# Sample attention: old keys turned in place on VectorE, scores on 32x32 array tiles, pairs of sequences one by one

## The chip, the core and the metric

The kernel runs on one core of a Trainium2 chip. The metric is the device time of one execution in microseconds (us): the median of three runs. One further execution was recorded by the hardware profiler, and its rows are what is read here. The engines are TensorE (PE in the rows, its weight loads PEld), VectorE (DVE), ScalarE (ACT), GpSimd (POOL) and SyncE (SP), whose queue issues the large transfers.

## The reference, cut to what matters

The program is one inference step of a two-layer decoder trunk. Every layer projects its input, mixes tokens in three ways side by side (dilated attention A with 8 heads of 64, an RWKV recurrence B, and sliding-window attention C with 16 query heads on 2 key heads), projects back and applies a gated feed-forward block. There is one prompt of 256 tokens, and there are 8 sample sequences with 8 new tokens each. A sample sequence attends to cached keys and values that were loaded from memory. For mixer A these are 1280 cached positions that its branches reach; for mixer C the last 128 positions. In short, for each sample sequence and head:

```python
s = einsum(q, concat(cached_k, new_k)) * HEAD_DIM ** -0.5   # masked by branch and distance
p = softmax(s)                                              # C: with a learned sink
o = einsum(p, concat(cached_v, new_v))
```

## The kernel before

All engines are programmed by hand; a named semaphore stands for each hand-over, and each engine takes its instructions in the order in which they are written. A layer runs the input projections, the RWKV stage, the attention of the prompt (24 units, loop over `u`), the attention of the samples, the output projection `out` and the feed-forward block. Tokens stand in the free dimension of `pT` (256 prompt columns, then 64 of samples).

The sample attention takes the eight sequences in four pairs, q = 0 to 3. The cached keys of a pair lie in `cK[0]` and `cK[1]`, the values in `cV[0]` and `cV[1]`: 128 partitions (positions) x 10 blocks x 512 columns (8 heads of 64) in float32, loaded in three pieces, called quads, of 4, 4 and 2 blocks. The last pair's values go to `cK[0]` and to `cX`. `ckc` and `cvc` hold the C keys and values of 128 positions.

A score needs the head dimension on the partitions, but the cache brings positions there. So TensorE first turns the keys:

- `keys(q)`: `turn` transposes 128x128 blocks of `cK` against an identity into two PSUM banks (82 a pair, with the two of `ckc`), ScalarE's `key_tiles` copies them to `ktr` (eight buffers, 26 copies a pair), and `score` multiplies them by the queries `qdA`, in four column tiles of 32 side by side. Then come the new keys: `pT,qdA` and `pT,qdC` in the rows.
- VectorE's `scores(q)` scales and masks the PSUM result into `smA` and `smC` and takes the maxima `snm`; ScalarE's `exps(q)` makes the exponentials and their sums `ssu`.
- `probabilities(q)`: TensorE transposes `smA` and `smC`, ScalarE copies them to `ptA` and `ptC`.
- `values(q)`: TensorE multiplies the new values (`tk`), the C values (`cvc`) and the cached values (`cV`) by them; VectorE's `weighted(q)` scales the result into `om` and `omC`.
- `select(q)`: TensorE gathers `om` and `omC`, and VectorE's `outputs(q)` writes them to `pT`.

TensorE's order is keys(0), then for each q keys(q+1), probabilities(q), values(q). The `select` of a pair stands within the keys of a later one. Semaphores in the rows: `s_bS` scores of a pair are in PSUM; `s_smb` VectorE has read them; `s_bnm` maxima are there; `s_bex` exponentials are there; `s_pvq` a piece of the values is done; `s_ktp`, `s_ktc` a block is turned, copied; `s_sc` a group of scores is done; `s_cK0` and the like: a quad has landed.

SyncE issues the keys of a next pair quad by quad, as `s_ktp` counts up, and the values as `s_pvq` does.

Of the kernel before, what the change touches and what calls it, by code (L numbers as in the profile page):

```python
# [31 lines left out]
ALU = mybir.AluOpType  # L32
# [5 lines left out]
P = 128  # L38
# [136 lines left out]
def build(nc, I, O, at):  # L175
    ctx = ExitStack()
    with ctx:
# [82 lines left out]
        ktr = [place(f"ktr{i}", [P, 512], RW + 40960 + 2048 * i if i < 3 else RK + 2048 * (i - 3)) for i in range(8)]  # L260
# [28 lines left out]
        def C(name, rows=P, cols=None):  # L289
# [4 lines left out]
        names = """con con2 x x1 xh xlo par lora s0 cK0 cK1 cK2 cV0 cV1 cV2 w0 w1 wh wl mm ev gexp  # L294
            xtr xtc sq ssum nmm hh part
            zero shc sht shrc th sg z aa zexp aexp g gc ksq kss rkp rks clr expd abkr bon st stc
            tok tokc mixq RKs G Gc et Z Zc TZ TW TA TAc NV NVc TNV U Uc Sm SP Y Yc mz mk U1 U1c ux Se SF So Soc
            gn gnc ysq gv vr sd rn gsd grn xs keep kf cl drr bl vx Sov TT WZ rk2 sqd ssd finr hpp qp qp0 et0 E1 NT RB tnv rw rot rotc kv kvc qz qbd
# [20 lines left out]
        TURNS, GROUPS = 26, 7  # L319

        def group_of(g):
            return g // TURNS * GROUPS + min(g % TURNS // 4, GROUPS - 1)

# [4 lines left out]
        def keys_in(l, q, quad):  # L328

            return sem[f"cK{quad}"], (304 if quad == 2 else 288) * l + 64 * (q + 1)  # L330

        def values_in(l, q, quad):

            if q == LASTQ:
                return sem[f"cK{quad}"], (304 if quad == 2 else 288) * (l + 1)
            return sem[f"cV{quad}"], 32 * (3 - quad) * (LASTQ * l + q + 1)

# [22 lines left out]
        def _(sp):  # L360
# [75 lines left out]
            for l in range(DEPTH):  # L436
# [12 lines left out]
                sp.wait_ge(sem["zero"], 2 * l + 3)  # L449
# [17 lines left out]
                def cache(b, which, quad):  # L467

                    last = which == "V" and b // 2 == LASTQ
                    s = sem[f"c{'K' if last else which}{quad}"]  # L470
# [19 lines left out]
                for which in "KV":  # L490
                    for quad in range(3):
                        cache(0, which, quad)
                        cache(1, which, quad)
# [15 lines left out]
                def next_keys(q):  # L509
                    for quad in range(3):  # L510
                        sp.wait_ge(sem["ktp"], TURNS * (4 * l + q - 1) + (8 * (quad + 1) if quad < 2 else TURNS))
                        cache(2 * q, "K", quad)
                        cache(2 * q + 1, "K", quad)

                def next_values(q):
                    for quad in range(3):
                        if q < LASTQ:
                            sp.wait_ge(sem["pvq"], 3 * (4 * l + q - 1) + quad + 1)
                        else:
                            sp.wait_ge(sem["ktp"], TURNS * (4 * l + q) + (8 * (quad + 1) if quad < 2 else TURNS))  # L520
                        cache(2 * q, "V", quad)
                        if q < LASTQ:
                            cache(2 * q + 1, "V", quad)
                        elif quad == 2:
                            sp.dma_start(ckc[1][:], I["cache_c_v"][l, NB - 1].rearrange("r h d -> r (h d)")).then_inc(sem["cK2"], 16)
                next_keys(1)
                next_keys(2)
                next_values(1)
                next_keys(3)
                next_values(2)  # L530
                next_values(3)
# [7 lines left out]
            for tau, need in enumerate((1, 0, 2)):  # L539
# [14 lines left out]
        def _(pool):  # L554
# [9 lines left out]
            for l in range(DEPTH):  # L564
# [3 lines left out]
                pool.wait_ge(sem["pool"], l + 1)  # L568
# [18 lines left out]
                pool.memset(mkb[1][:], 0.0).then_inc(sem["mz"], 1)  # L587

                pool.wait_ge(sem["SF"], 4 * (l + 1))
                pool.wait_ge(sem["rope"], 9 * (l + 1))  # L590
                for i in range(4):
                    pool.memset(qp[i][:], 0.0).then_inc(sem["qp0"], 1)
                for u in range(24):

                    if u:
                        pool.wait_ge(sem["qp"], 24 * l + u)
                    else:
                        pool.wait_ge(sem["qp0"], 4 * (l + 1))
# [9 lines left out]
                z.then_inc(sem["qz"], 1)  # L608
                pool.wait_ge(sem["qz"], l + 1)
                pool.wait_ge(sem["rope"], 9 * (l + 1))  # L610
# [19 lines left out]
        def _(act):  # L630
# [155 lines left out]
            for l in range(DEPTH):  # L786
# [62 lines left out]

                for u in range(24 + 3):  # L850
# [24 lines left out]
                def key_tiles(q):  # L875
                    for t in range(TURNS):
                        if q == 1 and t in (4, 8):
                            exps(0, t == 4)
                        g = TURNS * (4 * l + q) + t
                        n = QUADS[t // 8][1] * P if t < 24 else P  # L880
                        take("ktp")
                        if g >= 8:
                            act.wait_ge(sem["sc"], group_of(g - 8) + 1)
                        act.activation(ktr[g % 8][:, 0:n], PS[:, 4 + g % 2, 0:n], ACT.Copy).then_inc(sem["ktc"], 1)  # L884

                def exps(q, first=None):

                    i = q % 2
                    if first in (None, True):
                        take("bnm")  # L890
                        act.activation(smA[i][:], smA[i][:], ACT.Exp, bias=snm[i][:, 0:1], accum_out=ssu[i][:, 0:1])
                    if first in (None, False):
                        for b2 in range(2):
                            act.activation(smC[i][:, b2], smC[i][:, b2], ACT.Exp, bias=snm[i][:, 1 + b2:2 + b2], accum_out=ssu[i][:, 1 + b2:2 + b2])
                        act.activation(ssk[i][:], snm[i][:, 1:3], ACT.Exp, bias=snk[:, 0:1]).then_inc(sem["bex"], 1)

                act.wait_ge(sem["snk"], 16 * (l + 1))
                key_tiles(0)
                for q in range(NB // 2):
                    if q < NB // 2 - 1:  # L900
                        key_tiles(q + 1)
                    if q == 0:
                        act.wait_ge(sem["out"], 16 * 12 * (l + 1))
                    for r in range(4):
                        take("pt2")
                        b0 = r if q == LASTQ else 6 + r % 2
# [11 lines left out]
                    if q < NB // 2 - 1:  # L918
                        exps(q + 1)

                act.wait_ge(sem["pvq"], 12 * l + 9)
                act.wait_ge(sem["ktp"], TURNS * 4 * (l + 1))
# [13 lines left out]
            act.wait_ge(sem["finr"], 1)  # L936
# [9 lines left out]
        def _(dve):  # L946
# [222 lines left out]
            def rwkv(l):  # L1169
                xk = xm[:, 4:8]  # L1170
                col = lambda r, f: par[:, r + f:r + f + 1]
                dve.wait_ge(sem["zero"], 2 * l + 2)
# [3 lines left out]
                for tau in range(3):  # L1176
# [40 lines left out]
                    for c in range(2) if tau < 2 else range(1):  # L1217
# [3 lines left out]
                        else:  # L1221
                            dve.wait_ge(sem["TAc"], 3 * (l + 1))
                            take("mz")
# [72 lines left out]
            def attention(l):  # L1296
# [20 lines left out]

                def scores(q):
# [5 lines left out]
                    for k in range(3):  # L1324
                        n = 512 if k < 2 else 256
                        stt(x[:, 512 * k:512 * k + n], PS[:, k, 0:n], SCALE, C("oldA")[:, 512 * k:512 * k + n], ALU.mult, ALU.add)
                    stt(x[:, 1280:1344], PS[:, 2, 256:320], SCALE, C("newA")[:, 64 * q:64 * q + 64], ALU.mult, ALU.add)
                    ps = PS[:, 3, 0:384].rearrange("p (b k) -> p b k", b=2)
# [5 lines left out]
                def weighted(q):  # L1334
# [7 lines left out]
                    stt(v3(om[:]), v3(PS[:, 6, 0:256]), ssu[i][:, 0:1], C("headof").unsqueeze(2).broadcast_to([P, 4, HD]), ALU.mult, ALU.mult)  # L1342
                    for b2 in range(2):
                        a = stt(omC[:, b2], PS[:, 7, b2 * P:(b2 + 1) * P], ssu[i][:, 1 + b2:2 + b2], C("headones"), ALU.mult, ALU.mult)
# [679 lines left out]
```

## Time and profile before

| what | value |
|---|---|
| median of 3 runs | 3399.21 us (3396.51 to 3399.39) |
| the profiled execution's own time | 3401.5 us |
| its span in the profile | 3399.6 us |
| TensorE busy | 3272.0 us, 96% of the span |
| VectorE busy | 1711.3 us, 50% |
| ScalarE busy | 1208.5 us, 36% |

The span is the time from the first to the last recorded instruction. Matmul ends are modelled, so a busy TensorE is not TensorE at its peak. The shares are averages over stages with different limits. The stage that the change touches stands once in each layer, in the first from 528.4 us on and in the second from 2201.8 us on.

### The profile page before, as it was taken

How to read it: one execution, taken by the hardware profiler on the slowest of the kernel's cores; microseconds unless marked ns; L12 is line 12 of the kernel's file. 1: busy time of each engine (PE TensorE's matmuls, PEld its weight loads, DVE VectorE, ACT ScalarE, POOL GpSimd, SP SyncE). 2: the span in 40 equal slices, each digit the busy share in tenths (PEclk: the TensorE clock that was granted, in tenths of full speed). 3: DMA queues.
4: the chain of work that ended last, by engine and by line, in shares of the span. 5: the costliest groups of instructions: out<-in, count | busy, mean ns of one | idle time of the engine just before them, and what ended most of it. 6: DMA issues, size and time to landing. Idle time of an engine off the chain costs nothing.

```text
span 3399.6 us, 60962 instructions
## 1 busy us (share of the span) xinstructions
PE 3272.0 (96%) x25078; PEld 3074.4 (90%) x25078; DVE 1711.3 (50%) x2269; ACT 1208.5 (36%) x1607; POOL 91.9 (3%) x209
## 2 busy tenths in 40 slices
PE   7999888999999999999999988889999999999998
PEld 6999755699999999999999986557999999999998
DVE  5455572355555454454545664714555544545544
ACT  3332256433322222222434313654422323323234
POOL 1000011000000000000000000100000000000000
PEclk9999889999999999999999998999999999999999
DMA  6552036765555554554564610577655545545454
GB/s 196 164 135 65 2 132 234 258 151 150 150 150 140 159 148 138 160 148 140 152 190 136 137 27 2 191 278 201 148 149 151 149 140 164 149 136 161 137 146 132
DMA packets 848704, 501.17 MB, mean 147 GB/s; under 512 B 96608, under 2 KB 823152, under 8 KB 848112
## 3 DMA queue, kind: packets, MB, share of 16 engines
q1 hardware_dynamic: 848108, 499.01, 51.7%
q8 instruction: 106, 1.74, 0.2%
q14 instruction: 38, 0.31, 0.0%
q10 hardware_dynamic: 452, 0.11, 0.0%
HBM read 485.71 MB, written 13.37 MB: 147 GB/s over the span
## 4 chain that ended last, share of the span: by engine, by line
PE 91%; DVE 4%; ACT 2%; issue 1%; DMA 1%; ACTq 0%; SPq 0%; DVEq 0%
PE PS L1435 87%; PE PS L1436 4%; ACT ktr L884 1%; ACT psm L855 0%; DVE psm L1303 0%; DVE wl L962 0%; ACT ppt L866 0%; DVE nm L1305 0%; ACT wh L641 0%; DVE S0T L1255 0%; DMA sink<-in_c_sink 0%; DVE rt L1080 0%; DMA raw<-in_w_out 0%; DVE WT L1183 0%; DMA raw<-in_w_in 0%
## 5 line engine op out<-in xcount | busy, mean ns | idle before, releaser
L641 ACT ACTIVATE wh<-raw 128x2048 fp32r<-128x2048 f32 (+1 forms) x408 | 711.7, 1744 | 1235.7 <-PE PS L1435 1214.2
L962 DVE TENSOR_TENSOR wl<-raw,wh 128x2048 fp32r<-128x2048 f32 (+1 forms) x408 | 848.9, 2081 | 400.2 <-ACT wh L641 399.6
L1435 PE MATMUL PS<-fh,wh 128*128 128x320 f32 x2816 | 870.6, 309 | 0.0
L1435 PE MATMUL PS<-fh,wl 128*128 128x320 f32 x2816 | 870.1, 309 | 0.0
L1435 PE MATMUL PS<-fl,wh 128*128 128x320 f32 x2816 | 870.1, 309 | 0.0
L1435 PEld LDWEIGHTS PS<-fh,wh 128*128 128x128 f32 x2816 | 528.5, 188 | 0.2
L1435 PEld LDWEIGHTS PS<-fl,wh 128*128 128x128 f32 x2816 | 528.5, 188 | 0.2
L1435 PEld LDWEIGHTS PS<-fh,wl 128*128 128x128 f32 x2816 | 528.5, 188 | 0.0
L1435 PE MATMUL PS<-hh,wh 128*128 128x320 f32 (+2 forms) x1696 | 521.3, 314 | 4.8 <-DVE wl L962 4.8
L1435 PE MATMUL PS<-hh,wl 128*128 128x320 f32 (+2 forms) x1696 | 513.5, 309 | 0.0
L1435 PE MATMUL PS<-hl,wh 128*128 128x320 f32 x1664 | 510.5, 310 | 0.0
L1435 PE MATMUL PS<-ah,wh 128*128 128x320 f32 x1408 | 435.7, 309 | 0.2 <-DVE wl L962 0.2
L1435 PE MATMUL PS<-al,wh 128*128 128x320 f32 x1408 | 435.1, 309 | 0.0
L1435 PE MATMUL PS<-ah,wl 128*128 128x320 f32 x1408 | 435.1, 309 | 0.0
L1435 PEld LDWEIGHTS PS<-hh,wh 128*128 128x128 f32 x1696 | 317.9, 191 | 8.6 <-DVE wl L962 5.2
L1435 PEld LDWEIGHTS PS<-hh,wl 128*128 128x128 f32 x1696 | 315.2, 189 | 0.0
L1435 PEld LDWEIGHTS PS<-hl,wh 128*128 128x128 f32 x1664 | 312.2, 188 | 1.4
L1435 PEld LDWEIGHTS PS<-ah,wh 128*128 128x128 f32 x1408 | 264.3, 188 | 0.8 <-issue 0.5
L1435 PEld LDWEIGHTS PS<-al,wh 128*128 128x128 f32 x1408 | 264.3, 188 | 0.0
L1435 PEld LDWEIGHTS PS<-ah,wl 128*128 128x128 f32 x1408 | 264.3, 188 | 0.0
L670 ACT ACTIVATE ge<-gt 128x320 f32<-128x320 f32 x88 | 41.5, 472 | 488.2 <-DVE gt L1002 488.2
L1002 DVE TENSOR_TENSOR gt<-PS,rsb 128x320 f32<-128x320 f32 x88 | 43.3, 492 | 224.7 <-PE PS L1435 224.6
(329 smaller groups left out, 2711.4 us busy)
## 6 DMA issues: line engine op xcount, KB each, us to landing
raw<-in_w_gate SPq DMA_DIRECT2D x88, 1024.0 KB, 5.6
raw<-in_w_up SPq DMA_DIRECT2D x88, 1024.0 KB, 5.6
raw<-in_w_down SPq DMA_DIRECT2D x128, 704.0 KB, 4.8
raw<-in_w_in SPq DMA_DIRECT2D x56, 1024.0 KB, 5.6
cK<-in_cache_a_k SPq DMA_DIRECT2D x80, 512.0 KB, 6.5
cV<-in_cache_a_v SPq DMA_DIRECT2D x60, 512.0 KB, 8.8
raw<-in_w_in SPq DMA_DIRECT2D x32, 512.0 KB, 5.3
raw<-in_w_out SPq DMA_DIRECT2D x32, 512.0 KB, 4.5
```

The source lines that it names most:

```text
L641: act.activation(wh[j][:, 0:kts], raw[j][:, 0:kts], ACT.Copy).then_inc(sem["wh"], 1)
L670: act.activation(ge[:], gt[:], ACT.Tanh, scale=0.5).then_inc(sem["gexp"], 1)
L884: act.activation(ktr[g % 8][:, 0:n], PS[:, 4 + g % 2, 0:n], ACT.Copy).then_inc(sem["ktc"], 1)
L962: tt(wl[j][:, 0:kts], raw[j][:, 0:kts], wh[j][:, 0:kts].bitcast(F32), ALU.subtract).then_inc(sem["wl"], 1)
L1002: tt(gt[:], PS[:, 0, 0:TOK], rsb[:], ALU.mult).then_inc(sem["ev"], 1)
L1435: mm = lambda out, lhsT, rhs, start=True, stop=True: pe.matmul(out, lhsT, rhs, start=start, stop=stop, skip_group_check=True)
L1436: tr = lambda out, x: pe.transpose(out, x, con[0:x.shape[0], at["ident"][0]:at["ident"][0] + x.shape[0]])
```

## The change

VectorE's new `turn(q)` transposes the loaded keys in place, in blocks of 32x32, with six instructions a pair (128x2048, 128x2048 and 128x1024 for each sequence). A 32x32 block then has 32 columns of a head on 32 partitions, and TensorE scores such blocks: a 32x32 tile of queries `qd` against 320 moving columns, with four row groups (`i`) times two column groups (`fh`), in four PSUM banks. The eight parts of a sum (four heads, two halves of a head) are accumulated in one bank. The queries have to lie on all four groups of 32 partitions: `query_rows(q)` brings them there by 16 small matmuls against the identity and eight ScalarE copies into `qd`, two buffers that GpSimd clears. The one for pair 0 stands ahead of the prompt attention.

```diff
+                def turn(q):
+
+                    for b2 in range(2):
+                        for quad, (k0, n) in enumerate(QUADS):
+                            dve.wait_ge(*keys_in(l, q, quad, b2))
+                            x = cK[b2][:, k0:k0 + n].rearrange("p k c -> p (k c)")
+                            dve.transpose(x, x).then_inc(sem["kt"], 1)
...
+                    old = lambda z: z[:, 0:1280].rearrange("p (k i c) -> p i k c", k=10, i=4)
+                    for r in range(4):
+                        stt(old(x)[:, r], PS[:, 4 + r, 0:320].rearrange("p (k c) -> p k c", k=10), SCALE, old(C("oldA"))[:, r], ALU.mult, ALU.add)
...
+                turn(0)
                 scores(0)
                 for q in range(NB // 2):
-                    if q:
-                        outputs(q - 1)
                     if q < NB // 2 - 1:
-                        scores(q + 1)
+                        turn(q + 1)
                     else:
                         split(start_of(l, "out"), 0, KT)
                     weighted(q)
+                    if q < NB // 2 - 1:
+                        scores(q + 1)
+                        outputs(q)
...
+                def query_rows(q):
+
+                    o = SEQ + 2 * TS * q
+                    for g in range(4):
+                        r = slice(32 * g, 32 * g + 32)
+                        for i in range(4):
+                            a = mm(PS[32 * i:32 * i + 32, 4 + g, 448:512].rearrange("p (f t) -> p f t", f=4), C("ident")[r, r], pT[r, QA:QA + 4, o:o + 2 * TS])
+                    a.then_inc(sem["ktp"], 1)
+                query_rows(0)
+                pe.wait_ge(sem["ktc"], 12 * l + 1)
                 for u in range(24 + 3):
...
                 def keys(q):
 
-                    for t in range(4):
-                        turn(q, t)
-                    take("qbd")
                     if q:
                         pe.wait_ge(sem["smb"], 4 * l + q)
-                    for group in range(GROUPS):
-                        for t in range(4 * group + 4, min(4 * group + 8, TURNS)):
-                            turn(q, t)
-                        if group == 3 and q >= 2:
-                            select(q - 2)
-                        score(q, group)
+                    window_keys(q)
+                    take("qbd")
+                    pe.wait_ge(sem["ktc"], 12 * l + 3 * q + 1)
+                    for b2 in range(2):
+                        pe.wait_ge(sem["kt"], 6 * (4 * l + q) + 3 * (b2 + 1))
+                        for h in range(4):
+                            for jj in range(2):
+                                for i in range(4):
+                                    r = slice(32 * i, 32 * i + 32)
...
+                                    for fh in range(2):
+                                        out = PS[64 * b2 + 32 * fh:64 * b2 + 32 * fh + 32, 4 + i, 0:320].rearrange("p (k c) -> p k c", k=10)
+                                        c0 = (4 * fh + h) * HD + 32 * jj
+                                        a = mm(out, qd[q % 2][r, b2, jj, fh, 32 * h:32 * h + 32], cK[b2][r, :, c0:c0 + 32], not (h or jj), h == 3 and jj == 1)
+                        a.then_inc(sem["sc"], 1)
...
-                keys(0)
                 for q in range(NB // 2):
+                    keys(q)
+                    if q:
+                        select(q - 1)
                     if q < NB // 2 - 1:
-                        keys(q + 1)
-                        probabilities(q)
-                    else:
-                        probabilities(q)
-                        select(q - 1)
+                        pe.wait_ge(sem["smb"], 4 * l + q + 1)
+                        query_rows(q + 1)
+                    probabilities(q)
                     values(q)
```

ScalarE's `key_tiles` goes. In its place are two copies of the turned C keys into `kcT` and, for the next pair, the eight of `query_rows`, both ahead of `exps(q)`. SyncE now asks for the next keys of a sequence when its scores are done (`s_sc`), in the order next_keys(q), next_values(q). The results of `values` move from PSUM banks 6 and 7 to banks 2 and 3. The rest renames semaphores.

Two places show how the order moves. The first is TensorE around the hand-over from a pair's keys to transposed probabilities. In the kernel before, at the end of pair 1's keys (`ktr`, `qdA_152`, `qdC_154` are of pair 1, `smA_165` of pair 0):

```order
L1435 MATMUL PS<-ktr_142,qdA_152 32x256
L1435 MATMUL PS<-ktr_143,qdC_154 128x128 [waits s_ktc]
L1435 MATMUL PS<-ktr_144,qdC_154 128x128
L1435 MATMUL PS<-pT,qdA_152 128x64 x4
L1435 MATMUL PS<-pT,qdC_154 128x64 x2
L1436 MATMUL PS<-con,smA_165 128x128 [waits s_bex]
L1436 MATMUL PS<-con,smA_165 128x128 x7
L1436 MATMUL PS<-con,smA_165 128x128 [waits s_ptd]
```

In the changed kernel, right behind the 128 tile matmuls of pair 1's old keys (`smA_162` is of pair 1, `om` and `omC` are of pair 0, `pT,con` is the query rows of pair 2):

```order
L1444 MATMUL PS<-pT,qdA_148 128x64 [waits s_ktc]
L1444 MATMUL PS<-pT,qdA_148 128x64 x3
L1444 MATMUL PS<-kcT_141,qdC_150 128x128
L1444 MATMUL PS<-pT,qdC_150 128x64
L1444 MATMUL PS<-kcT_142,qdC_150 128x128
L1444 MATMUL PS<-pT,qdC_150 128x64
L1444 MATMUL PS<-con,om 128x32 [waits s_om]
L1444 MATMUL PS<-con,om 128x32
L1444 MATMUL PS<-con,omC 128x64 x2
L1444 MATMUL PS<-pT,con 32x64 [waits s_smb]
L1444 MATMUL PS<-pT,con 32x64 x15
L1445 MATMUL PS<-con,smA_162 128x128 [waits s_bex]
```

Before, pair 0's probabilities stood behind the whole of pair 1's keys. Now a pair's probabilities stand behind its own scores, with only `select` of the pair before and the 16 matmuls of the query rows between them and the wait for the exponentials (`s_bex`).

The second place is VectorE after the maxima of a pair. In the kernel before, between the maxima of pair 1 (`snm_188`) and the scores of pair 2:

```order
L1331 TENSOR_REDUCE snm_188<-smA_166 128x1 [waits s_smb]
L1332 TENSOR_REDUCE snm_188<-smC_168 128x2
L1338 TENSOR_TENSOR ssu_189<-ssu_189,ssk_191 128x2 [waits s_bex,s_bnm]
L1339 RECIPROCAL ssu_189<-ssu_189 128x3 [waits s_dve]
L1342 SCALAR_TENSOR_TENSOR om<-PS,ssu_189,con 128x256 [waits s_pvq,s_dve]
L1344 SCALAR_TENSOR_TENSOR omC<-PS,ssu_189,con 128x128 x2
L1351 COPY pT<-PS 128x2x16 [waits s_sel,s_om]
L1351 COPY pT<-PS 128x2x16
L1354 COPY pT<-PS 128x8x8 x2
L1326 SCALAR_TENSOR_TENSOR smA_165<-PS,con 128x512 [waits s_pt2,s_bS,s_bo]
```

In the changed kernel, between the maxima of pair 0 (`snm_183`) and the scores of pair 1:

```order
L1339 TENSOR_REDUCE snm_183<-smC_163 128x2
L1323 STREAM_TRANSPOSE cK_139<-cK_139 128x2048 [waits s_cK00,s_bnm]
L1323 STREAM_TRANSPOSE cK_139<-cK_139 128x2048 [waits s_cK10]
L1323 STREAM_TRANSPOSE cK_139<-cK_139 128x1024 [waits s_cK20]
L1323 STREAM_TRANSPOSE cK_140<-cK_140 128x2048 [waits s_cK01]
L1323 STREAM_TRANSPOSE cK_140<-cK_140 128x2048 [waits s_cK11]
L1323 STREAM_TRANSPOSE cK_140<-cK_140 128x1024 [waits s_cK21]
L1345 TENSOR_TENSOR ssu_185<-ssu_185,ssk_187 128x2 [waits s_bex]
L1346 RECIPROCAL ssu_185<-ssu_185 128x3 [waits s_dve]
L1349 SCALAR_TENSOR_TENSOR om<-PS,ssu_185,con 128x256 [waits s_pvq,s_dve]
L1351 SCALAR_TENSOR_TENSOR omC<-PS,ssu_185,con 128x128 x2
L1333 SCALAR_TENSOR_TENSOR smA_162<-PS,con 128x10x32 [waits s_bS,s_om]
```

The six transposes of the next pair stand ahead of this pair's sums and weighted values, which stand ahead of the next pair's scores.

## Rows read from the trace of the kernel before

**Rows 1.** Page, the chain that ended last: shares of the span.

```profile
PE 91%; DVE 4%; ACT 2%; issue 1%; DMA 1%; ACTq 0%; SPq 0%; DVEq 0%
```

**Rows 2.** Stretches of the stage: us, then each engine's busy us, PEclk, DMA share, GB/s.

```profile
528.40:549.40 21.00, 18.68 (x147) 11.43 (x148) 0.00 (x0) 12.14 (x27) 0.00 (x0) 1.00 0.62 215
549.40:575.00 25.60, 21.25 (x149) 12.92 (x148) 4.29 (x8) 14.50 (x33) 1.93 (x12) 0.87 0.60 211
...
605.80:636.50 30.70, 27.91 (x267) 17.43 (x266) 6.18 (x17) 16.63 (x39) 0.00 (x0) 1.00 0.88 330
...
2201.80:2331.30 129.50, 114.04 (x1052) 70.57 (x1052) 25.01 (x60) 70.88 (x161) 3.85 (x24) 0.97 0.71 248
```

**Rows 3.** TensorE's timeline, one pair: start, us, operation, count, idle before and releaser.

```profile
584.47 1.09 PE L1436 MATMUL PS<-con,cK 128*128 128x128 f32 x8
...
598.92 0.53 PE L1435 MATMUL PS<-con,om 128*128 128x32 f32 x4
...
599.86 1.07 PE L1435 MATMUL PS<-ktr,qdA 128*32 128x512 f32 x8
...
603.92 0.71 PE L1435 MATMUL PS<-ktr,qdC 128*128 128x128 f32 x4
...
605.75 1.04 PE L1436 MATMUL PS<-con,smA 128*128 128x128 f32 x8
...
608.92 0.64 PE L1435 MATMUL PS<-tk,ptA 64*32 64x256 f32 x8 [0.73 <-ACT ptC L916]
...
610.77 4.52 PE L1435 MATMUL PS<-cV,ptA 128*32 128x256 f32 x80
615.23 0.98 PE L1436 MATMUL PS<-con,cK 128*128 128x128 f32 x7
```

**Rows 4.** VectorE's timeline, the scores of a pair.

```profile
606.02 1.62 DVE L1326 SCALAR_TENSOR_TENSOR smA<-PS,con 128x512 f32<-128x512 f32 x3 [5.43 <-issue]
...
608.33 1.55 DVE L1331 TENSOR_REDUCE snm<-smA 128x1 f32<-128x1344 f32 x1
609.80 0.54 DVE L1332 TENSOR_REDUCE snm<-smC 128x2 f32<-128x384 f32 x1
```

**Rows 5.** ScalarE's timeline, first and last of the seven exponential instructions.

```profile
579.57 1.42 ACT L891 ACTIVATE smA<-smA,snm 128x1344 f32<-128x1344 f32 x1 [1.45 <-DVE snm L1332]
...
581.86 0.28 ACT L895 ACTIVATE ssk<-snm,snk 128x2 f32<-128x2 f32 x1
```

**Rows 6.** TensorE's timeline, the last pair of layer 0.

```profile
645.99 1.42 PE L1436 MATMUL PS<-con,smA 128*128 128x128 f32 x11
...
648.77 0.64 PE L1435 MATMUL PS<-tk,ptA 64*32 64x256 f32 x8
...
658.72 1.06 PE L1435 MATMUL PS<-con,om 128*128 128x32 f32 x4 [3.44 <-DVE omC L1344]
```

**Rows 7.** VectorE's timeline, the end of the stage in layer 0.

```profile
655.05 2.29 DVE L962 TENSOR_TENSOR wl<-raw,wh 128x2048 fp32r<-128x2048 f32 x1 [5.72 <-ACT wh L641]
657.26 0.15 DVE L1338 TENSOR_TENSOR ssu<-ssu,ssk 128x2 f32<-128x2 f32 x1
```

**Rows 8.** TensorE's timeline, 64x64 array tiles in the RWKV stage.

```profile
310.07 0.65 PE L1435 MATMUL PS<-dB,dA 64*64 64x64 f32 x32
310.53 0.65 PE L1435 MATMUL PS<-dA,dK 64*64 64x64 f32 x32
```

**Rows 9.** Stretches of layer 0, same columns as in rows 2.

```profile
551.60:555.00 3.40, 1.26 (x10) 0.84 (x8) 2.35 (x4) 1.81 (x3) 0.00 (x0) 1.00 0.23 83
555.00:561.80 6.80, 5.74 (x25) 3.51 (x26) 0.00 (x0) 4.34 (x12) 0.00 (x0) 0.50 0.32 100
...
588.00:600.00 12.00, 10.99 (x87) 6.68 (x89) 0.00 (x0) 7.74 (x16) 0.00 (x0) 1.00 1.01 399
```

**Rows 10.** TensorE's timeline, a wait in layer 0, and values in layer 1.

```profile
556.06 1.97 PE L1436 MATMUL PS<-con,cK 128*128 128x128 f32 x8 [2.91 <-ACT ktr L884]
...
2252.91 5.43 PE L1435 MATMUL PS<-cV,ptA 128*32 128x256 f32 x80
```

More of the change, by code:

```diff
@@ L259, in build @@
         cK = [place(f"cK{i}", [P, 10, 512], (RH if i == 0 else RW) + 20480) for i in range(2)]
-        ktr = [place(f"ktr{i}", [P, 512], RW + 40960 + 2048 * i if i < 3 else RK + 2048 * (i - 3)) for i in range(8)]
+        kcT = [place(f"kcT{i}", [P, P], RW + 40960 + 512 * i) for i in range(2)]
+        qd = [place(f"qd{i}", [P, 2, 2, 2, 160], RK + 5120 * i) for i in range(2)]
         cX = place("cX", [P, 10, 512], RX)
@@ L489, in _ @@
                 sp.wait_ge(sem["souts"], 16 * 18 * (l + 1))
-                for which in "KV":
+                for b2 in range(2):
                     for quad in range(3):
-                        cache(0, which, quad)
-                        cache(1, which, quad)
+                        cache(b2, "K", quad)
+                for quad in range(3):
+                    cache(0, "V", quad)
+                    cache(1, "V", quad)
                 for quad in range(3):
@@ L524, in next_values @@
                         elif quad == 2:
[L525 to L531, printed above, removed]
+                            sp.dma_start(ckc[1][:], I["cache_c_v"][l, NB - 1].rearrange("r h d -> r (h d)")).then_inc(sem["cK21"], 16)
+                for q in range(1, NB // 2):
+                    next_keys(q)
+                    next_values(q)
                 sp.wait_ge(sem["out"], 16 * 12 * (l + 1))
@@ L538, in _ @@
                         params(l + 1, i - 1)
-            for tau, need in enumerate((1, 0, 2)):
+            for tau, need in enumerate((2, 0, 3)):
                 if need:
@@ L886, in exps @@
[L886 to L895, printed above, removed]
@@ L897, in _, with exps @@
-                act.wait_ge(sem["snk"], 16 * (l + 1))
-                key_tiles(0)
-                for q in range(NB // 2):
+                def exps(q):
+                    i = q % 2
+                    take("bnm")
+                    act.activation(smA[i][:], smA[i][:], ACT.Exp, bias=snm[i][:, 0:1], accum_out=ssu[i][:, 0:1])
+                    for b2 in range(2):
+                        act.activation(smC[i][:, b2], smC[i][:, b2], ACT.Exp, bias=snm[i][:, 1 + b2:2 + b2], accum_out=ssu[i][:, 1 + b2:2 + b2])
+                    act.activation(ssk[i][:], snm[i][:, 1:3], ACT.Exp, bias=snk[:, 0:1]).then_inc(sem["bex"], 1)
@@ L900, in _ @@
+                act.wait_ge(sem["snk"], 16 * (l + 1))
+                for q in range(NB // 2):
+                    for b2 in range(2):
+                        take("ktp")
+                        act.activation(kcT[b2][:], PS[:, 6 + b2, 320:448], ACT.Copy).then_inc(sem["ktc"], 1)
                     if q < NB // 2 - 1:
-                        key_tiles(q + 1)
+                        query_rows(q + 1)
+                    exps(q)
                     if q == 0:
```

169 lines of the change are left out of this document (72 added, 97 removed).

## The prediction

> **What bounds the kernel now.** I read the page first: the chain that ended last runs through TensorE for 91% of the span, VectorE has 4% and ScalarE 2% of it [rows 1]. So only what TensorE does, or waits for, moves the end. Next comes the table by stretches of the stage that the change touches. The sample attention of layer 0 lasts from the last copy of the prompt attention at 528.4 to the last `weighted`, which starts at 657.26: 128.9 us [rows 2, 7]. That of layer 1 takes 129.5 us. TensorE is busy in 27.91 of 30.70 us of a pair and in 114.04 of the 129.50 us of layer 1 [rows 2]. The stage is thus a row of TensorE work with small gaps.
>
> One pair in TensorE's timeline shows what that work is [rows 3]: from 584.47 to 605.75 keys are turned and scored (21.3 us), to 608.92 probabilities are turned (3.2 us), to 615.23 values are weighted (6.3 us). The period is 30.8 us. While TensorE does the next pair's keys, VectorE and ScalarE make this pair's scores and exponentials: VectorE needs 4.3 us from 606.02 to 610.34 [rows 4], ScalarE 2.6 us from 579.57 to 582.14 [rows 5]. These 7 us cost nothing now, since TensorE has other work.
>
> **What the change does to one pair.** It takes 82 transposes with their 26 copies off TensorE and ScalarE, gives VectorE six block transposes instead, and has TensorE score on 32x32 tiles. By the order, TensorE now does keys(q), select(q-1), query_rows(q+1), probabilities(q), values(q). 
>
> *Scores and exponentials, now on the path: 7.1 us.* VectorE 4.3 us; four pieces of 320 columns stand for three of 512, 512 and 256, at about the same count. ScalarE 2.6 us, and 0.2 us of semaphores. Under the two reductions (2.1 us, from 608.33 on [rows 4]) TensorE and ScalarE make the next query rows: 16 small matmuls (about 0.4 us) and eight small copies. I take 0.18 us for a copy, a little below the 0.28 us of the smallest activation [rows 5], since they overlap; 1.9 us in all, just covered.
>
> *Probabilities 3.2 us, values 6.3 us*, as before [rows 3].
>
> *Next keys: 11.5 us.* Two transposes of the window keys, a copy and its semaphore: 0.9 us. The tile scores are 128 matmuls a pair with 320 columns. How fast they go is not in this trace; the nearest rows are these. The 80 records of the value matmuls, four tiles side by side with 256 columns, take 4.52 us [rows 3], so 0.213 us for a round of four (20 rounds, 0.2 us to drain). In a 64x64 group, 32 records of 64 columns take 0.46 us from one start to the next [rows 8]; at the rate just found a record alone would need 0.053 us, so 3.7 of them ran at once, on row and column groups. The spacing of 0.0145 us also shows that issue is no bound: eight tiles of 320 columns need a matmul only every 0.033 us. If eight run together, 256 records are 32 rounds of 0.266 us, 8.5 us a pair; if four, 17.0 us. I take eight, as row groups and column groups both ran together in the 64x64 group. New keys take the 1.8 us of 603.92 to 605.75 [rows 3], and the ends 0.3 us.
>
> That is 28.1 us, 2.7 us less than now, but with TensorE standing for 7 us in each pair.
>
> *The clock.* The one wait like it in the trace: TensorE is busy 1.26 of 3.40 us at 551.6 to 555.0, and in the 6.80 us after it the granted clock is 0.50, the low level of 1.2 GHz [rows 9]. It cost about 2.3 us: the stretch from 549.4 to 575.0 took 25.6 us [rows 2], against 21.3 us of a later pair less 0.95 us of `select` (598.92 to 599.86 [rows 3]) and plus the wait of 2.91 us for a `ktr` copy [rows 10]. A slighter fall at the same work in layer 1 is seen in value matmuls of 5.43 us instead of 4.52 us [rows 3, 10], about 1.1 us with the matmuls ahead of them. Most it can cost by these rows is 3.4 us, half of 6.8. I take 2.7 us, between 2.3 and 3.4, since the waits are longer than that one; it falls on probabilities and values.
>
> The Trainium skill, TensorE: Matmul & The Clock Gate, HAM oscillation, says that TensorE's waits bring its clock down and that a loop which waits in every round pays for it in every round. Here it speaks against the change; by it all eight waits pay, as I assume, while this trace shows one full fall.
>
> *VectorE's block transposes.* No such instruction is in the trace. Neighbours of like size: a reduction of 1344 elements in 1.55 us [rows 4], so 2.4 us for 2048, and a product over 2048 columns in 2.29 us [rows 7]. I take 2.25 us for 2048 and 1.15 us for 1024: 5.6 us for a sequence, 11.2 us a pair. Twice that is my upper end. In the middle pairs it lies under the chain: it starts when scores(q) end, 4.4 us after `bS`, and ends at 15.6 us, while the chain asks for the first sequence at 17.5 us and the second at 21.8 us. `weighted(q)` stands behind it on VectorE, wanted at 16.6 us and not waited for by TensorE until `select` after the next keys.
>
> The Trainium skill, Vector Engine (DVE) Microarchitecture Reference, 3.8, states one element a cycle for this transpose. An estimate from it at 0.96 GHz is 2.1 us for 2048; the sum would be 0.5 us a layer shorter, at the start. No row shows it.
>
> *Transfers.* Keys of the next pair are now asked for when a sequence has been scored, not during the turning. Keys of a pair are 5.2 MB, at the 399 GB/s of a full stretch [rows 9] 13.1 us, values as much: 26.3 us in a period of 30.8 us. The first sequence's scores end about 6 us before `bS`, so its keys are there at about +5 and the second's at +11 to +12; VectorE is then still turning the first. The cover is some 6 us at TensorE.
>
> **The sum of a layer.** Start: VectorE turns both sequences (11.3 us), the second is scored (4.3 us), new keys follow (2.1 us), and 0.8 us for the low clock while TensorE waited for VectorE (if it held to the end it would be 2 us): 18.5 us to `bS`, where it is now 21.2 us. Three pairs at 28.1: 84.3 us. The last pair: 7.1 + 2.8 (645.99 to 648.77) + 6.5 (to 655.28, where the wait of 3.44 us begins) [rows 6] + 0.2: 16.6 us. Together 119.4 us with the clock held, 130.2 us with four falls of 2.7. The mean before is 129.2 us, which includes 2 us that the last `weighted` stood behind a weight product of 2.29 us [rows 7]; that one now finds VectorE free while values run. So +1.0 us a layer. Outside it: query_rows(0) stands before the prompt attention, with 8 copies that TensorE waits for, +1.9 us (1.2 to 2.6); the last `select`, at half clock before (1.06 us for a first group [rows 6]), comes after a shorter wait, -0.5 us (0 to -0.9). The two more clears on GpSimd lie in its idle time ahead of the prompt loop. A layer gets +2.4 us, the kernel +4.8 us. The profiled execution took 3401.5 us, 0.07% above the median of 3399.2; I add the change to the median: 3404.0 us.
>
> **The rivals.** The bound of what can be told from no change is 0.2%, 6.8 us.
>
> *The clock holds* (faster). Eight row and column tiles keep the array full for 8.5 us in each pair, which may bring the clock back or hold it over 7 us. Then 119.4 us a layer: 8 x 2.7 = 21.6 us less, 3382 us. Against it stands the one wait in rows 9. In between, half the loss (falls of 1.1 to 1.5 us, as in layer 1): 3393 us. The forecast turns into a gain that can be told once a fall costs under 1.2 us.
>
> *VectorE's transposes at half rate*: 22.4 us a pair. The turning would set the period: 4.4 + 22.4 + 4.3 + 2.2 = 33.3 us, and the start 29.7 us; 29.7 + 99.9 + 19.3 = 148.9 us a layer, 20 us more than now, 3441 us. Every 0.1 us more for a 2048 puts 0.5 us on each layer's start, and from 4.0 us on the turning sets the period. For it: reads and writes of one tile in place, of which no row tells anything.
>
> *Fewer than eight tiles at once.* Four at once add 8.5 us in each later pair and 7.0 us at the start (there the second sequence's scores follow at 14.1 us in place of 11.3): 3404 + 65 = 3469 us; six add 2.8 us a pair, 3427 us. For it: eight have never run here, 3.7 have. The Trainium skill, TensorE: Matmul & The Clock Gate, Part 3, has nine 32x32 tiles 6.32 times as fast as one; by that ratio eight are worth 5.6, an estimate of 3.6 us a pair and 3433 us for the kernel. The value rows, which lose nothing to packing, speak against it.
>
> *Keys late*: each wait that outlasts its cover by 2.5 us in the three later pairs gives 15 us, 3419 us. For it: the queue is already full for whole stretches (share 1.01 [rows 9]).
>
> **Chances.** Forecast 0.50, with 3394 to 3412 us its own range (falls of 1.4 to 3.4 us, query rows 1.2 to 2.6). Clock held 0.13, half held 0.11, half-rate transposes 0.11, fewer tiles 0.09, late keys 0.06. The range takes in the held clock and the half-rate case, 3380 to 3443, and leaves the fewest tiles and some of the edges out. Faster: 0.13, 0.06 of the half-held and 0.02 of the forecast, 0.21. Same: 0.31 of the forecast and 0.05, 0.36. Slower: 0.17 of it and the last three cases, 0.43.
>
> **What would show it.** A STREAM_TRANSPOSE of 128x2048 at 2.2 us; a group of 128 records on 32x32 tiles, for a sequence, in 4.3 us; TensorE idle for 6 to 7 us before each smA group, with VectorE's snm and ScalarE's exps as releasers; granted clock 0.5 in the slices behind it; a period of 30 to 31 us. Wrong it would be if the tile groups last 8 us, if TensorE waits for `kt` in the later pairs, or if value groups still take 4.5 us.

## The result, and the profile after

The changed kernel takes 3408.55 us (median of 6 runs, 3407.18 to 3413.49). Beside it the kernel before took 3397.5 us (6 runs, 3391.45 to 3399.39). The ratio is 1.0039, with a 95% interval of 1.0026 to 1.0052: 11 us slower. The profiled execution took 3408.06 us, with a span of 3406.3 us; that of before, at 3401.5 us, lay 4 us above its own median, so the two traces differ by 6.7 us only.

The page of the changed kernel, parts 1 and 4, gives the answer to [rows 1]. TensorE is busy 33 us less, yet the end comes later: VectorE's share of the chain rises from 4 to 5%, and "issue", time in which an engine waited for nothing that the profile shows, from 1 to 3%.

```profile
PE 3239.3 (95%) x26358; PEld 3060.6 (90%) x26358; DVE 1798.6 (53%) x2325; ACT 1125.7 (33%) x1479; POOL 96.7 (3%) x213
...
PE 90%; DVE 5%; issue 3%; ACT 2%; DMA 0%; ACTq 0%; DVEq 0%
```

TensorE's timeline of one pair (pair 2 of layer 0) answers to [rows 3]:

```profile
599.90 0.44 PE L1445 MATMUL PS<-con,ckc 128*128 128x128 f32 x2
600.27 8.97 PE L1444 MATMUL PS<-cK,qd 32*32 32x320 f32 x256
609.17 1.10 PE L1444 MATMUL PS<-pT,qdA 128*128 128x64 f32 x8
...
613.83 0.53 PE L1444 MATMUL PS<-pT,con 32*32 32x64 f32 x32 [1.60 <-DVE smC L1337]
618.48 2.70 PE L1445 MATMUL PS<-con,smA 128*128 128x128 f32 x11 [4.12 <-ACT ssk L893]
...
622.98 1.08 PE L1444 MATMUL PS<-tk,ptA 64*32 64x256 f32 x8 [0.73 <-ACT ptC L917]
...
626.28 6.67 PE L1444 MATMUL PS<-cV,ptA 128*32 128x256 f32 x80
632.89 0.44 PE L1445 MATMUL PS<-con,ckc 128*128 128x128 f32 x2
```

Window keys begin at 599.90, the scores of old keys take 8.97 us for 256 records, new keys follow until 611.3. Then TensorE has only `select` and the query rows (613.83) until 618.48, where the wait for the exponentials ends. Probabilities last until 622.98 (4.5 us where it was 3.2), values until 632.89 (9.9 us where it was 6.3). The period is 33.0 us, where it was 30.8. VectorE's timeline, which answers to [rows 4] and shows the new instruction:

```profile
530.51 11.14 DVE L1323 STREAM_TRANSPOSE cK<-cK 128x2048 f32<-128x2048 f32 x6 [2.51 <-PE PS L1444]
...
554.02 11.14 DVE L1323 STREAM_TRANSPOSE cK<-cK 128x2048 f32<-128x2048 f32 x6
...
587.21 2.31 DVE L1323 STREAM_TRANSPOSE cK<-cK 128x2048 f32<-128x2048 f32 x1 [0.18 <-DMA cK<-in_cache_a_k]
...
611.43 1.68 DVE L1333 SCALAR_TENSOR_TENSOR smA<-PS,con 128x320 f32<-128x320 f32 x4 [10.31 <-issue]
```

Six transposes take 11.14 us, one of 2048 columns 2.31 us. The second group (554.02) starts behind the maxima of pair 0 and ends at 565.16, long before the tile scores of pair 1 (569.93). The scores start after 10.31 us without work.

The clock shows in the table by stretches. Each row is one pair from the start of its probabilities to the end of its values, layer 0 first (columns: us, busy us of PE, PEld, DVE, ACT, POOL, granted clock PEclk, DMA share, GB/s). With TensorE at its high level such a row would be 9.5 us long, 9.3 in the last pair:

```profile
556.60:569.50 12.90, 12.12 (x111) 7.26 (x111) 8.78 (x7) 2.38 (x6) 0.00 (x0) 0.64 0.31 109
589.10:599.90 10.80, 10.06 (x111) 6.33 (x111) 9.65 (x8) 2.38 (x6) 0.00 (x0) 0.81 0.76 286
618.50:632.90 14.40, 13.67 (x112) 7.82 (x112) 11.55 (x8) 2.38 (x6) 0.00 (x0) 0.58 0.59 232
651.30:662.00 10.70, 9.95 (x111) 6.52 (x111) 2.54 (x3) 7.23 (x11) 0.00 (x0) 0.85 0.95 136
2230.20:2244.30 14.10, 13.35 (x111) 7.67 (x111) 8.76 (x7) 2.38 (x6) 0.00 (x0) 0.59 0.29 103
2265.00:2275.80 10.80, 10.07 (x112) 6.32 (x112) 9.37 (x7) 2.38 (x6) 0.00 (x0) 0.81 0.65 235
2296.60:2307.20 10.60, 9.87 (x112) 6.31 (x112) 9.53 (x8) 2.38 (x6) 0.00 (x0) 0.85 0.58 226
2325.60:2338.30 12.70, 11.93 (x111) 7.00 (x111) 2.54 (x3) 7.97 (x11) 0.00 (x0) 0.67 0.57 100
```

They add up to 97.0 us, 21.4 us more than eight rows without loss (six of 9.5 and two of 9.3 us). In four pairs only the probabilities ran at the low level (1.1 to 1.4 us lost), in the other four the values did in part as well (3.4 to 4.9 us).

One kind of wait was in no term of the sum. Rows of TensorE's timeline, tile scores of pair 1 in layer 0, then of pairs 1 and 2 in layer 1:

```profile
577.11 2.91 PE L1444 MATMUL PS<-cK,qd 32*32 32x320 f32 x75 [0.84 <-issue]
...
2244.68 6.39 PE L1444 MATMUL PS<-cK,qd 32*32 32x320 f32 x187
2253.00 2.88 PE L1444 MATMUL PS<-cK,qd 32*32 32x320 f32 x69 [1.94 <-issue]
...
2283.49 4.00 PE L1444 MATMUL PS<-cK,qd 32*32 32x320 f32 x111 [2.15 <-issue]
```

In pair 1 of layer 1 TensorE stood for 1.94 us in the middle of a row of matmuls, with no semaphore that ended the wait. Three such waits in tile scores (0.84 us in layer 0, 1.94 and 2.15 us in layer 1) come to 4.9 us; the trace of the kernel before has none. The stretches around the wait of 1.94 us, and beside them the tile scores of the last pair of layer 0, which had no such wait:

```profile
2244.60:2251.00 6.40, 6.40 (x189) 4.69 (x188) 0.94 (x3) 0.45 (x2) 0.00 (x0) 1.00 1.01 390
2251.00:2253.00 2.00, 0.06 (x5) 0.00 (x0) 0.00 (x0) 0.00 (x0) 0.00 (x0) 1.00 1.01 379
...
633.20:642.20 9.00, 9.00 (x259) 6.75 (x257) 0.92 (x3) 0.45 (x2) 0.00 (x0) 1.00 0.29 86
```

The transfer engines were full (1.01) when it happened and at 0.29 in the last pair.

What came ahead of the end of each wait is in the trace's records of single DMA packets, which give the queue, start and duration of each. Part 3 of the page names a queue that carries instructions (packets, MB, share of the 16 transfer engines):

```profile
q8 instruction: 116, 1.90, 0.2%
```

A packet of 16 KB of this queue landed at 575.64, 2251.52 and 2282.03 us, and TensorE went on 1.47, 1.48 and 1.46 us later. The experiment without values comes back to this.

The stage ends for layer 0 with `select`, which answers to the last of [rows 6] and now runs at the high level after a shorter wait:

```profile
663.19 0.63 PE L1444 MATMUL PS<-con,om 128*128 128x32 f32 x4 [1.20 <-DVE omC L1351]
```

From the last copy of the prompt attention to the last `select` layer 0 takes 132.9 us (530.31 to 663.19) where it took 130.3 us (528.4 to 658.72 [rows 2, 6]), and layer 1 134.6 us where it took 131.0 us: 6.2 us more in the profiled executions.

### The profile page after: what moved, and what is told of

The parts are those of the page before. It is cut to its first block, busy times and chain, and to the rows that moved or that the text cites. A ratio compares the mean times of both kernels' runs of the same rounds, so it can differ in the third digit from the quotient of the medians.

```text
span 3406.3 us, 63243 instructions
## 1 busy us (share of the span) xinstructions
PE 3239.3 (95%) x26358; PEld 3060.6 (90%) x26358; DVE 1798.6 (53%) x2325; ACT 1125.7 (33%) x1479; POOL 96.7 (3%) x213
## 4 chain that ended last, share of the span: by engine, by line
PE 90%; DVE 5%; issue 3%; ACT 2%; DMA 0%; ACTq 0%; DVEq 0%
PE PS L1444 87%; PE PS L1445 3%; ACT psm L866 0%; DVE psm L1302 0%; DVE smA L1333 0%; ACT smA L890 0%; DVE cK L1323 0%; ACT ppt L877 0%; DVE nm L1304 0%; DVE S0T L1254 0%; DMA sink<-in_c_sink 0%; ACT smC L892 0%; DVE rt L1079 0%; DMA raw<-in_w_in 0%; DVE wl L961 0%
```

## The experiments

The kernel before was timed again beside the experiments: 3398.2 us (31 runs) beside the fillers, the longer link, the query rows moved alone and the missing values, 3396.65 us (17 runs) beside the other three. Ratios are to it. Differences to the changed kernel are between medians (3408.55 us, ratio 1.0039, interval 1.0026 to 1.0052).

### Fillers in TensorE's waits

```diff
+                def warm(n):
+
+                    for i in range(n):
+                        mm(PS[:, i % 2, :], C("ident"), con[:, 0:512])
                 for q in range(NB // 2):
                     keys(q)
                     if q:
                         select(q - 1)
                     if q < NB // 2 - 1:
+                        warm(1)
                         pe.wait_ge(sem["smb"], 4 * l + q + 1)
                         query_rows(q + 1)
+                    warm(4 if q < NB // 2 - 1 else 6)
                     probabilities(q)
```

Four more stand behind `window_keys(0)`.

> The changed kernel with idle TensorE filled: matmuls of the identity with 512 constant columns into PSUM banks 0 and 1, whose results nothing reads, stand in the waits of the sample attention (4 before the first tile scores, 1 before and 4 behind the query rows of pairs 0 to 2, 6 before the last probabilities). Theory (the low clock behind each wait costs about 2.7 us a pair, 21 us in all): granted clock 1.00 in probabilities and values, 3.2 and 6.3 us for them in every pair, and a time near 3387 us. Rival 1 (the loss is the chain of waits alone, the clock costs little): no more than 3 us faster, near 3406 us. Rival 2 (the fillers delay the query rows or the probabilities on TensorE): slower than 3410 us, with a shorter wait for the exponentials and a later start of them.

Measured: 3388.91 us (10 runs), ratio 0.9974 (0.9963 to 0.9984): 20 us faster than the changed kernel, and faster than the kernel before by 0.26%. The same eight stretches, from probabilities to the end of values:

```profile
554.20:563.80 9.60, 8.54 (x112) 5.23 (x112) 8.75 (x7) 2.27 (x6) 0.00 (x0) 1.00 0.30 96
583.40:592.90 9.50, 8.50 (x111) 5.21 (x111) 8.26 (x5) 2.27 (x6) 0.00 (x0) 1.00 0.90 331
613.30:624.40 11.10, 10.11 (x112) 5.86 (x112) 9.66 (x8) 2.27 (x6) 0.00 (x0) 0.85 0.57 225
642.80:652.10 9.30, 8.36 (x111) 5.17 (x111) 2.54 (x3) 7.58 (x11) 0.00 (x0) 1.00 0.87 145
2220.50:2231.70 11.20, 10.12 (x111) 5.77 (x111) 8.77 (x7) 2.27 (x6) 0.00 (x0) 0.85 0.27 86
2250.60:2260.10 9.50, 8.51 (x111) 5.19 (x111) 8.29 (x5) 2.27 (x6) 0.00 (x0) 1.00 1.02 386
2280.10:2289.70 9.60, 8.56 (x112) 5.24 (x112) 8.13 (x5) 2.27 (x6) 0.00 (x0) 1.00 0.74 292
2308.10:2317.40 9.30, 8.35 (x111) 5.16 (x111) 2.10 (x1) 6.17 (x10) 0.00 (x0) 1.00 0.86 147
```

They add up to 79.1 us, 17.9 us less. Six of eight have the clock at 1.00 throughout, two lose 1.6 and 1.7 us. TensorE's timeline ahead of pair 1's probabilities:

```profile
578.77 0.41 PE L1444 MATMUL PS<-pT,con 32*32 32x64 f32 x32 [0.71 <-DVE smC L1337]
579.11 3.70 PE L1444 MATMUL PS<-con 128*128 128x512 f32 x8
583.42 1.09 PE L1445 MATMUL PS<-con,smA 128*128 128x128 f32 x8 [0.61 <-ACT ssk L893]
```

Behind the query rows (578.77) eight filler records take 3.70 us, and TensorE still waits 0.61 us for ScalarE's last exponential, so the fillers delay nothing. Both rivals fall: the clock was worth about 20 us.

### A longer link in the chain

```diff
+                    act.activation(pad[:], con[:, 0:1280], ACT.Copy)
                     act.activation(ssk[i][:], snm[i][:, 1:3], ACT.Exp, bias=snk[:, 0:1]).then_inc(sem["bex"], 1)
```

> The changed kernel with one more ScalarE copy of 1280 columns (about 1.35 us, into a buffer that nothing reads) behind the exponentials of each pair, ahead of their hand-over. Theory (scores and exponentials are one chain with TensorE in each pair): all of it is added, 8 x 1.3 = 10.5 us, near 3419 us. Rival (TensorE is held by something else in that wait, the transposes or the query rows): no more than 3 us, near 3410 us.

Measured: 3412.81 us (10 runs, 3404.28 to 3421.17), ratio 1.0045 (1.0030 to 1.0059): 4 us slower than the changed kernel by the medians, which does not stand clear of it, and nearer the rival's number. TensorE's timeline, probabilities of pairs 0 and 1:

```profile
556.91 2.76 PE L1447 MATMUL PS<-con,smA 128*128 128x128 f32 x11 [5.28 <-ACT ssk L895]
...
588.40 2.71 PE L1447 MATMUL PS<-con,smA 128*128 128x128 f32 x11 [5.40 <-ACT ssk L895]
```

The wait in front of them grew from 4.17 to 5.28 us and from 4.24 to 5.40 us. It grew by 1.1 to 1.2 us in all eight pairs, 9.2 us. So the link is on the chain; the rival's reason is wrong, though its number was nearer. From the last prompt copy to the last `select` the two layers together take 275.5 us (530.01 to 661.10 and 2200.17 to 2344.59), 8.0 us more than the 267.5 us of the changed kernel. Layer 0 got shorter in spite of the longer waits, 131.1 us, because the values of all four of its pairs ran at the high level, and layer 1 took 144.4 us. Ten runs spread over 17 us. How much of the clock a pair loses is thus not fixed by the length of its wait, and a median of this kernel hides a change of a few us. The eight stretches from probabilities to the end of values lose some 20 us here, 21.4 us in the changed kernel, and some 30 and 29 us in the traces of the next experiment and of the one without values, where the waits in front of them are those of the changed kernel.

### Query rows of pair 0 behind the prompt attention

```diff
-                query_rows(0)
-                pe.wait_ge(sem["ktc"], 12 * l + 1)
                 for u in range(24 + 3):
...
                 pe.wait_ge(sem["oc"], 24 * (l + 1))
+                query_rows(0)
+                pe.wait_ge(sem["ktc"], 12 * l + 1)
```

ScalarE's eight copies move in the same way, behind its part of the prompt loop.

> The changed kernel with query_rows(0) moved from ahead of the prompt attention to the wait for VectorE's first block transposes, which TensorE spends idle (5.1 us). Theory (query_rows(0) stands on the path ahead of the prompt loop, about 1.5 us a layer): 3 us faster, near 3405.5 us, and the first tile scores start at the same time after the prompt's last copy. Rival (the prompt loop waits there for the last state copies and ScalarE's table anyway): no change, 3408.5 us.

Measured: 3410.19 us (10 runs), ratio 1.0034 (1.0023 to 1.0046): no difference that shows. In place it does what was expected. TensorE's timeline at the start of layer 0's prompt attention, changed kernel first, then the moved one:

```profile
466.07 0.60 PE L1445 MATMUL PS<-con,S0P 128*128 128x128 f32 x4
...
468.75 2.56 PE L1444 MATMUL PS<-pT,qp 128*128 128x128 f32 x12 [1.10 <-ACT qd L857]
```

```profile
464.65 0.60 PE L1445 MATMUL PS<-con,S0P 128*128 128x128 f32 x4
465.82 2.53 PE L1444 MATMUL PS<-pT,qp 128*128 128x128 f32 x12 [0.57 <-ACT SoutP L847]
```

From the last state transposes to the first prompt matmul it is 2.68 us in the one and 1.17 us in the other, 1.51 us less, and the same in layer 1. To see it without the clock's scatter I repeated it with the fillers.

> Fillers as in the first experiment, together with query_rows(0) moved behind the prompt attention. Theory (query_rows(0) costs 1.5 us a layer ahead of the prompt loop, and the unresolved result without fillers was the clock's scatter): 3 us faster than the fillers alone, near 3386 us. Rival (moving it gains nothing, since its 1.5 us come back ahead of the first tile scores or in the clock of the prompt loop): 3389 us.

Measured: 3391.2 us (9 runs, 3385.67 to 3394.64), ratio 0.9977 (0.9968 to 0.9987); the fillers alone had 0.9974. The rival's number held. The 1.51 us are gained at that place and are not seen at the end; medians of 9 and 10 runs with a spread of 9 us can't tell 3 us apart. The traces do not settle it either. From the start of the last state transposes to that of the last prompt matmuls the two layers take 122.0 us with the fillers alone and 122.1 us with the move, but 123.8 us in the changed kernel and 121.8 us with the move and no fillers. Whether the prompt loop gives the 1.51 us back stays open.

### No values for pairs 1 and 2

The loads of the cached values of two pairs are left out, so their values are those of pair 0.

```diff
                         if q < LASTQ:
                             sp.wait_ge(sem["pvq"], 3 * (4 * l + q - 1) + quad + 1)
+                            continue
                         cache(2 * q, "V", quad)
-                        if q < LASTQ:
-                            cache(2 * q + 1, "V", quad)
-                        elif quad == 2:
+                        if quad == 2:
```

> The changed kernel without the loads of cached values for pairs 1 and 2 (their values are those of pair 0), 21 MB less in the two layers. Theory (the waits of 0.84, 1.94 and 2.15 us inside the tile scores, which no semaphore ends, are TensorE's instructions arriving late behind full transfer queues): no such wait is left, about 5 us faster, near 3403.5 us. Rival 1 (these waits come from the many short instructions themselves): they stay, 3408 us. Rival 2 (late keys hold the transposes and so TensorE): TensorE's start of the tile scores moves forward in the later pairs, over 8 us faster.

Measured: 3403.9 us (10 runs), ratio 1.0014 (1.0004 to 1.0024): 4.7 us less than the changed kernel. Two of the four stretches of tile scores in which the changed kernel could have waited:

```profile
570.00:579.10 9.10, 9.10 (x259) 6.85 (x258) 0.91 (x3) 0.45 (x2) 0.00 (x0) 1.00 0.27 93
...
2242.60:2251.70 9.10, 9.10 (x259) 6.87 (x258) 0.92 (x3) 0.45 (x2) 0.00 (x0) 1.00 0.29 97
```

TensorE is busy in all of the 9.10 us of each of the four, and the transfer engines in 0.26 to 0.29 of them. The waits inside the tile scores are gone with the traffic, as the theory had it, and both rivals fall: the waits did not stay, and in pairs 1 to 3 TensorE's tile scores start right behind the window keys in both kernels.

That these waits are for instructions is borne out by the times of the packets of queue q8. In the three pairs that waited, its packet started 4.7, 5.8 and 4.9 us after the first tile score; without the traffic it started 2.2, 2.3 and 1.3 us after, and nothing waited. All 20 waits in the tile scores of six kernels (the changed one, three with fillers, the longer link, and the query rows moved alone) ended 1.23 to 1.49 us after such a packet had landed. In the three of these kernels without fillers they lie behind the same records, the 181st of pair 1 in layer 0 and the 187th of pair 1 and 145th of pair 2 in layer 1, though these come at other times in each. That the queue brings TensorE's instructions is read from this lag; the trace does not name the engine.

The 4.7 us are not a measure of the waits. In the profiled execution the stage takes 268.3 us for both layers, 0.8 us more than in the changed kernel, because its pairs lost 8 us more in clock.

### Transposes made twice

Each block transpose is made twice, so the keys are scored unturned.

```diff
-                            dve.transpose(x, x).then_inc(sem["kt"], 1)
+                            done(dve.transpose(x, x))
+                            dve.transpose(x, x).then_inc(sem["kt"], 1)
```

> The changed kernel with every block transpose on VectorE made twice, so that the keys are scored unturned (the scores are not the reference's). A pair then needs 22.3 us on VectorE. Theory (in pairs 1 to 3 the transposes lie under the chain, with some 6 us of cover for TensorE): the start of a layer grows by 11 us, and each later pair by the part of 11 us that outlasts the cover, 4 to 6 us, less 2 to 3 us where TensorE's later start takes the half clock's loss out of the path: 22 + 6 x 3 = 40 us, near 3448 us. Rival (the transposes are on the path in every pair now): 8 x 11 = 89 us, near 3497 us.

Measured: 3455.63 us (4 runs), ratio 1.0171 (1.0156 to 1.0187): 47 us slower than the changed kernel. TensorE's timeline, tile scores of pair 0 (both sequences) and of the second sequence of pairs 1 and 3 in layer 0:

```profile
540.80 6.73 PE L1445 MATMUL PS<-cK,qd 32*32 32x320 f32 x128 [11.05 <-DVE cK L1324]
552.20 6.16 PE L1445 MATMUL PS<-cK,qd 32*32 32x320 f32 x128 [4.66 <-DVE cK L1324]
...
587.88 4.67 PE L1445 MATMUL PS<-cK,qd 32*32 32x320 f32 x128 [0.81 <-DVE cK L1324]
...
657.84 6.23 PE L1445 MATMUL PS<-cK,qd 32*32 32x320 f32 x128 [4.94 <-DVE cK L1324]
```

The start of layer 0 grows by 12.2 us (from the turning of the window keys to `bS` 31.0 us where it was 18.8), that of layer 1 by 13.1 us. In the six later pairs TensorE waits for VectorE by 0.8 to 4.9 us, 11.0 us in all, of the 66 us that were added there. So the transposes had 6 to 10 us of cover in every later pair, and the rival (89 us) falls. Starts and waits make 36.3 us. Most of the rest is clock: the eight stretches from probabilities to the end of values add up to 108.0 us, 11 us more than in the changed kernel. Tile scores behind the new waits can be slow too (6.23 us in pair 3 for what takes 4.5).

### One more filler

The last kernel has query_rows(0) late, the fillers, and one more filler of 256 columns ahead of `values`.

```diff
+                    mm(PS[:, 6, 0:256], C("ident"), con[:, 0:256])
                     pe.wait_ge(sem["ptd"], 4 * (4 * l + q) + 4)
```

> The kernel of the run before with one more filler of 256 columns ahead of the wait for the last copied probabilities in each pair (0.73 us of waiting). Theory (in two pairs of eight the clock still fell behind the probabilities, 1 to 2 us each): values take 6.3 us in all pairs, 2 to 3 us faster than without. Rival (a filler there delays the values by what the wait does not cover): the values start later by 0.1 to 0.3 us in each pair, the same time or 2 us slower.

Measured: 3388.3 us (9 runs, 3381.62 to 3394.8), ratio 0.9975 (0.9964 to 0.9985). TensorE's timeline of pair 2 in layer 0:

```profile
611.86 0.64 PE L1444 MATMUL PS<-tk,ptA 64*32 64x256 f32 x8 [0.30 <-ACT ptC L917]
...
613.70 4.52 PE L1444 MATMUL PS<-cV,ptA 128*32 128x256 f32 x80
```

TensorE now waits 0.30 us of the 0.73 us, and values take 6.3 us in this pair and in all seven others. But in two pairs (pair 2 of layer 0, pair 1 of layer 1) the fillers themselves ran at the low level and the probabilities started 0.8 us later than in the others. The profiled execution took 3385.42 us, the shortest of all that were profiled, but the median does not stand clear of 3391.2 us without that filler. Shown in place, not shown in the time.

## Why the prediction came out as it did

The direction and the reason were right: forecast 3404.0 us and slower rather than faster, measured 3408.55 us. The change of 4.8 us was measured as 11 us, so the size was off. Step by step:

- **Scores and exponentials on the path, 7.1 us a pair.** Right: from `bS` (611.3) to the first transposed `smA` (618.48) it is 7.1 us, and the copy added there lengthened the wait in every pair.
- **Tiles, eight at once, 8.5 us.** Right in kind, small by size: 8.97 us, 0.27 us for a round of eight where 0.266 was taken, and the 0.2 us at the end left out. It does not lengthen the sum, because the window keys took 0.37 us where 0.9 was counted: the next keys as a whole took 11.3 to 11.4 us where nothing held them up, against 11.5 forecast. Two errors cancelled there, which was luck. That only four run at once is ruled out: at the rate taken 8.97 us is 7.6 of 8. The Trainium skill's page TensorE: Matmul & The Clock Gate, Part 3, has the ratio by which eight were estimated at 5.6; that ratio is not what limits eight tiles here.
- **Clock, 2.7 us a pair.** Near in the sum, 21.4 us where 21.6 was taken, but not in the single pair: pairs lost 1.1 to 1.4 or 3.4 to 4.9 us, and the most that a fall was said to cost was 3.4 us. In three pairs the value groups still took 4.52 us, which the prediction itself named as a sign that it was wrong. That the sum agrees so well is luck, for in the traces of kernels with like waits it lies between 20 and 30 us. The fillers show that it is the clock and not the wait that took these microseconds. The Trainium skill says in TensorE: Matmul & The Clock Gate, HAM oscillation, that a wait in each round costs clock in each round. The trace agrees: all eight pairs lost some.
- **Transposes, 11.2 us a pair, covered.** Right: 11.14 us, with 6 to 10 us of cover. A transpose of 2048 columns took 2.31 us, 2.25 was taken. The estimate of 2.1 us from the Trainium skill's Vector Engine (DVE) Microarchitecture Reference, 3.8, was a little low.
- **Keys late.** Did not happen at TensorE. VectorE waited for keys in pairs 2 and 3, up to 1.93 us, under the cover.
- **Start of a layer, 18.5 us.** From the last prompt copy to `bS` 19.2 us in layer 0 and 18.2 us in layer 1.
- **Query rows ahead of the prompt, 1.9 us.** 1.51 us.
- **What failed: a term was missing.** The sum counted transfers as a matter of keys coming in time, and nothing for what a full queue does to TensorE's own instructions. 128 tile matmuls in a row, with the queues full, met waits of 4.9 us in all, and without the traffic none. With this, less 0.8 us for the query rows, the sum is 4.8 + 4.9 - 0.8 = 8.9 us. The two traces differ by 6.7 us and the medians by 11 us (9 to 18 us by the interval of the ratio). The clock alone moves by 10 us between traces of kernels with like waits, so what is left is not resolved.

The two stages took 261.3 us before and 267.5 us after in the profiled executions; without the clock's loss of 21.4 us it would be 246 us, and with fillers it took 247.4 us (529.25 to 653.29 and 2195.57 to 2318.97). So with the clock held the stage is some 14 us shorter than before, waits included, and without the fillers the one chain loses more than that again in clock. The changed kernel with the fillers is faster than either: 3388.9 us.

## What to carry to other kernels

Work that is moved off TensorE saves its time only if TensorE has something else to do; where it waits in each round, price the clock behind the wait and the wait apart: here the clock alone turned a gain of 14 us into a loss. If the wait must stay, matmuls that nothing reads, sized to end before the awaited semaphore, can give the clock back: here 20 us. Count a long row of short instructions as something that full transfer queues can hold up, here by up to 2.2 us. Look at a term in each round, not in its sum alone: here errors cancelled.

## What the runs showed of the hardware that was not expected

- In the changed kernel TensorE stopped for 0.8 to 2.2 us inside rows of tile matmuls, with no semaphore to wait for, only in stretches where the transfer engines were full (share 0.99 to 1.04), and not in every one of them; at a share of 0.3 never. It went on 1.23 to 1.49 us after a 16 KB packet of an instruction queue had landed, in all 20 such waits of six kernels.
- The same wait of 4.1 to 4.3 us behind the same work cost between 1.1 and 4.9 us of clock in different pairs of one execution. With the longer link, waits of 5.3 to 7.4 us did not cost more in layer 0: all four pairs there lost 1.1 to 1.4 us.
- Eight 32x32 tiles of the array on four row and two column groups run together at nearly the full rate: 256 records of 320 columns in 8.97 us.
